# One 512-column fp32r matmul per direction for the decay rows of an mLSTM mixer, with operands of 128 rows in place of 64

## The chip, the cores and the metric

The kernel runs on one core of a Trainium2 chip. The metric is the device time of one execution in microseconds (us), as the median of several runs. The work is latency-bound inference of a small batch: 256 tokens of 1024 numbers, with about 320 MB of float32 weights that are read from HBM once.

## The reference, cut to what matters

Two layers: the first is a bidirectional mLSTM mixer and a PEER feed-forward part, the second a differential attention mixer and another PEER part. The change is in the first mixer. In one direction and for one head it computes, in chunks,

```python
D = b[..., :, None] - b[..., None, :] + li[..., None, :]     # decay from s to t
D = jnp.where(mask, D, -jnp.inf)
m_t = jnp.maximum(g, jnp.max(D, axis=-1))
Sqk = jnp.einsum('bhctd,bhcsd->bhcts', q, k) * jnp.exp(D - m_t[..., None])
num = jnp.einsum('bhcts,bhcsv->bhctv', Sqk, v) + ...          # state of the chunks before
h = num / jnp.maximum(jnp.abs(den), jnp.exp(-m_t))[..., None]
```

and h_fwd + h_bwd goes on, normalised by head, gated by sigmoid(o), and through w_out. The kernel does without chunks: it treats all 256 positions as one, so that for each head and direction there is one 256 x 256 matrix exp(A_s - M_t), masked, times the scores k_s.q_t, and one product with v.

## The kernel before, in words

**Weights.** All weight matrices are one stream of 128 x 1024 units (512 KB), in the order in which TensorE uses them: gate (1 unit), qk (8), vo (16), wo0 (8), wq0 (16), u0 and v0 (128 each), then the second layer's. SyncE loads each unit into a ring of four slots (`raw`). ScalarE rounds it to fp32r (`wh`, L465), VectorE makes the rest (`wl = raw - wh`, L826), and TensorE multiplies with both, so that three fast fp32r products stand for one float32 product. ScalarE and VectorE go ahead of TensorE by three units; the calls `ahead(unit)` in their programs say at which point the next unit is split. TensorE adds to the semaphore `used` behind each unit, and that frees the slot.

**The order of work is written out by hand** for each engine, in program order, with semaphores between the engines. There is no planner around the change.

**Start of the first mixer.** After the first norm, VectorE splits its units, clears three small tiles (L893 to L895; `zrow` is a row of zeros that a scan at L933 uses later, on partitions 0 to 15), copies the transposed gate projection out of PSUM (L897, `gT`), and TensorE transposes `gT` back between the first two qk units (L1530). The gates' logarithms are summed on 16 partitions (8 heads, 2 directions), and the results are turned into `colC` and `colD` (per token, one column per head and direction) and into `rowM`: for each direction and head the row -M_t over the 256 tokens. `rowM` has 64 rows in fp32r: rows 0 to 31 hold the rounded values, rows 32 to 63 what rounding left (L962, L963). `pick` (L948, L949) has 16 columns with ones in row c and row 32 + c, so that `pick[:, c]` as stationary operand, repeated over 128 columns, times `rowM` gives row c, to nearly full float32 precision, on all 128 partitions.

**The heads.** TensorE's loop over the eight heads (L1629) is: `o_unit(h)`, one weight unit of the gate o (12 matmuls of 512 columns, L1502 to L1504); `ml_decay(h + 1)`; after odd h `ml_scores` of the next two heads (L1596, 64-row float32 matmuls); `ml_values(h)` (L1622, six float32 products, which the profile shows as twelve matmuls). Before the loop stand `ml_decay(0)` and `ml_scores(0)`. In `ml_decay`, for each direction (PSUM bank 2 forward, bank 3 backward) and each half s of the source tokens, one fp32r matmul of 64 rows and 256 columns writes the picked row (L1609), and one bf16 matmul of 128 columns adds the triangle of -1e30 to the diagonal block (L1611):

```python
for b, c, m in ((2, h, mask_f), (3, 8 + h, mask_b)):
    for s in range(NT):
        at_ = s * S + s * P
        pe.matmul(ps[:, b, s * S:(s + 1) * S], pick[0:64, c:c + 1].to_broadcast([64, P]), rowM[0:64, :],
                  start=True, stop=False)
        i = pe.matmul(ps[:, b, at_:at_ + P], ident_b[:], m[:], start=False, stop=True)
i.then_inc(decay_mm, 1)
```

`ml_exp` on ScalarE (L549 to L552) waits for `decay_mm` and takes exp of the banks with the token's column of `colC` or `colD` as bias; `ml_weights` on VectorE (L975) multiplies by the scores; `ml_den` (L986 to L995) makes the denominators of the head before, ScalarE scales its forward part (L558), and `ml_output` (L1002) adds the backward part and signals `hs_ready`, for which `ml_values` of the next head waits. In heads 5 and 6 VectorE also gates finished heads (`ml_gate`, L1011), in head 6 it prepares the norm (L857), and in head 7 it scales the first four heads (L873), which TensorE then transposes (L1452). `v_block` (L944) copies v out of the banks that the first decay block then overwrites.

The full-width weight passes elsewhere serve the prediction as measures: `up_both_halves` (L1483 to L1486, fp32r, 128 rows, 512 and 256 columns), `weights` in the feed-forward part (L1678, f16, 128 rows, 64 columns), `keep_warm` (L1431, bf16, 512 columns, one operand repeated by a zero step), and the small products L1530 (32 rows) and L1580 (64 stationary columns).

Of the kernel before, what the change touches and what calls it, by code (L numbers as in the profile page):

```python
# [44 lines left out]
P = 128  # L45
S = 256
D = 1024
NT = S // P
# [51 lines left out]
def program(nc, stream, small, keys0, keys1, positions, x_in, out):  # L100
    with ExitStack() as ctx:
        def sb(name, shape, dt=F32):
            return ctx.enter_context(nc.sbuf_tensor(name, shape, dt))
# [4 lines left out]
        ps = ctx.enter_context(nc.psum_tensor("ps", [P, 8, 512], F32))  # L108
# [13 lines left out]
        ident_b = sb("ident_b", [P, P], BF16)  # L122
# [13 lines left out]
        rowM = sb("rowM", [P, S], F32R)  # L136
        pick = sb("pick", [P, 16], F32R)

        def area(at, *shape, dt=F32):

            n = int(np.prod(shape))
            v = big[:, at:at + (n // 2 if dt in (BF16, F16) else n)]
            if dt != F32:
                v = v.bitcast(dt)
            names = "abcd"[:len(shape)]
            if len(shape) > 1:
                v = v.rearrange(f"p ({' '.join(names)}) -> p {' '.join(names)}",
                                **{k: s for k, s in zip(names, shape)})
            return v
# [19 lines left out]
        zrow = area(18160, S)  # L169
# [613 lines left out]
        def _(dve):  # L783
            steps = [0]

            def chain(ins):

                steps[0] += 1
                ins.then_inc(dve_step, 1)
                dve.wait_ge(dve_step, steps[0])  # L790
# [100 lines left out]
            transposed(0, gain(0))  # L891
            ahead(0)
            dve.memset(v_ml[:, :, :, P:P + 1], 1.0)  # L893
            dve.memset(zrow[0:16, :], 0.0)
            chain(dve.memset(lgate[:], 0.0))  # L895
            dve.wait_ge(used, unit_of["gate"] + 1)
            dve.tensor_copy(gT[0:32, :], ps[0:32, 7, 0:S]).then_inc(gT_ready, 1)  # L897
            ahead(unit_of["qk"])
# [12 lines left out]
            for t in range(NT):  # L911
                i = dve.scalar_tensor_tensor(out=ftmp[:, 0, t], in0=g4[:, t, :, 1, :], scalar=-1.0,
                                             in1=g4[:, t, :, 1, :], op0=ALU.mult, op1=ALU.max)
# [8 lines left out]
            for d in range(2):  # L922
                i = dve.scalar_tensor_tensor(out=lgate[:, :, 2 + d, 8 * d:8 * d + 8], in0=g4[:, :, d, 1, :], scalar=0.0,
                                             in1=ftmp[:, 2, :, d, :], op0=ALU.min, op1=ALU.subtract)
# [32 lines left out]
            for d, col in ((0, colC), (8, colD)):  # L957
                i = dve.tensor_copy(colM[:, :, 0:3:2, d:d + 8],
                                    col[:, :, 16 + d:24 + d].unsqueeze(2).to_broadcast([P, NT, 2, 8]))
# [322 lines left out]
            for k in range(ROPE_HALF):  # L1282
                i = dve.tensor_scalar(trig[:, 1, :, k], trig[:, 0, :, 0], float(ROPE_INV[k]), None, ALU.mult)
# [138 lines left out]
        def _(pe):  # L1422
# [118 lines left out]
            for k in range(2):  # L1541
                for t in range(NT):
                    at_ = k * S + t * P
                    pe.matmul(ps[0:16, 7, at_:at_ + P], lgate[:, t, 2 * k, :], ident[:], start=True, stop=False)
                    i = pe.matmul(ps[0:16, 7, at_:at_ + P], lgate[:, 1 - t, 2 * k + 1, :], flip[:],
                                  start=False, stop=True)
# [19 lines left out]
            for t in range(NT):  # L1566
                for k in range(3):
                    at_ = t * 48 + k * 16
                    i = pe.matmul(ps[:, 7, at_:at_ + 16], rows[0:16, k, t * P:(t + 1) * P], ident[0:16, 0:16],
                                  start=True, stop=True)  # L1570
# [3 lines left out]
            for t in range(NT):  # L1574
                i = pe.matmul(ps[:, 7, t * 48:(t + 1) * 48], flip[:], colC[:, 1 - t, :], start=True, stop=True)
# [3 lines left out]
            for t in range(NT):  # L1579
                i = pe.matmul(ps[0:64, 7, t * P:(t + 1) * P], colM[:, t].rearrange("p r c -> p (r c)"), ident[:],  # L1580
                              start=True, stop=True)
# [18 lines left out]
            def ml_decay(h):  # L1600

                if h == 0:
                    pe.wait_ge(v_out, 4)
                else:
                    pe.wait_ge(e_ready, h)
                for b, c, m in ((2, h, mask_f), (3, 8 + h, mask_b)):
                    for s in range(NT):
                        at_ = s * S + s * P
                        pe.matmul(ps[:, b, s * S:(s + 1) * S], pick[0:64, c:c + 1].to_broadcast([64, P]), rowM[0:64, :],  # L1609
                                  start=True, stop=False)  # L1610
                        i = pe.matmul(ps[:, b, at_:at_ + P], ident_b[:], m[:], start=False, stop=True)  # L1611
                i.then_inc(decay_mm, 1)

            def ml_values(h):
# [10 lines left out]
                i.then_inc(av_mm, 1)  # L1625

            ml_decay(0)
            ml_scores(0)
            for h in range(HEADS):  # L1629
                o_unit(h)  # L1630
                if h + 1 < HEADS:
                    ml_decay(h + 1)
                if h % 2 == 1 and h + 1 < HEADS:
                    ml_scores((h + 1) // 2)
                if h == HEADS - 1:
                    pe.wait_ge(e_ready, HEADS)
                    for pair in range(2):
                        head_transposes(1, pair)
                ml_values(h)
# [246 lines left out]
```

## Time and profile before

| | |
|---|---|
| median of three runs | 1892.0 us (1890.98 to 1892.17) |
| the profiled execution's own time | 1889.36 us |
| its span | 1887.6 us |
| mean granted TensorE clock | 0.997 of full |
| busy: TensorE, VectorE, ScalarE, GpSimd | 99%, 76%, 52%, 6% |
| HBM traffic | 325 MB, 172 GB/s over the span |
| the eight heads of the first mixer | from 68.7 to 123.2 us |

The profile is of one execution. A matmul's record covers its way through the array, so records overlap; where TensorE is never idle, the distance between two starts tells what a matmul costs. "PEld" is the load of the stationary operand, which can run beside the matmul ahead of it.

### The profile page before, as it was taken

How to read it: one execution, taken by the hardware profiler on the slowest of the kernel's cores; microseconds unless marked ns; L12 is line 12 of the kernel's file. 1: busy time of each engine (PE TensorE's matmuls, PEld its weight loads, DVE VectorE, ACT ScalarE, POOL GpSimd, SP SyncE). 2: the span in 40 equal slices, each digit the busy share in tenths (PEclk: the TensorE clock that was granted, in tenths of full speed). 3: DMA queues.
4: the chain of work that ended last, by engine and by line, in shares of the span. 5: the costliest groups of instructions: out<-in, count | busy, mean ns of one | idle time of the engine just before them, and what ended most of it. 6: DMA issues, size and time to landing. Idle time of an engine off the chain costs nothing.

```text
span 1887.6 us, 33014 instructions
## 1 busy us (share of the span) xinstructions
PE 1862.8 (99%) x11274; PEld 1563.4 (83%) x11274; DVE 1428.1 (76%) x2630; ACT 978.9 (52%) x1398; POOL 105.9 (6%) x71
## 2 busy tenths in 40 slices
PE   8999999999999999999999999999999999999998
PEld 6778888888888888888876688888888888888887
DVE  5566588988888888655578756889888888885555
ACT  5465555655554444444466655555555444444444
POOL 0000342000000000000000003410000000000000
PEclk9999999999999999999999999999999999999999
DMA  6335455555555555555554244555555555555554
GB/s 228 123 112 167 156 191 189 177 172 175 171 174 179 176 173 173 190 193 192 193 175 137 88 159 163 182 189 178 178 178 170 171 172 172 174 176 195 194 193 163
DMA packets 89487, 326.13 MB, mean 173 GB/s; under 512 B 10065, under 2 KB 10193, under 8 KB 89041
## 3 DMA queue, kind: packets, MB, share of 16 engines
q1 hardware_dynamic: 88848, 323.00, 52.4%
q10 hardware_dynamic: 576, 2.33, 0.3%
q8 instruction: 35, 0.57, 0.1%
q14 instruction: 28, 0.22, 0.0%
HBM read 324.24 MB, written 1.05 MB: 172 GB/s over the span
## 4 chain that ended last, share of the span: by engine, by line
PE 94%; DVE 3%; ACT 2%; issue 0%; DMA 0%; DVEq 0%; ACTq 0%
PE ps L1486 25%; PE ps L1484 14%; PE ps L1730 12%; PE ps L1732 12%; PE ps L1731 12%; PE ps L1483 4%; PE ps L1678 3%; PE ps L1502 2%; PE ps L1504 2%; PE ps L1503 2%; DVE wl L826 1%; PE ps L1659 1%; PE ps L1622 1%; PE ps L1609 1%; ACT big L483 0%; ACT big L752 0%
## 5 line engine op out<-in xcount | busy, mean ns | idle before, releaser
L826 DVE TENSOR_TENSOR wl<-raw,wh 128x1024 fp32r<-128x1024 f32 x572 | 699.5, 1226 | 167.9 <-ACT wh L465 159.2
L465 ACT ACTIVATE wh<-raw 128x1024 fp32r<-128x1024 f32 x612 | 644.9, 1055 | 323.5 <-PE ps L1732 171.1
L1486 PE MATMUL ps<-hT,wh 128*128 128x512 f32 x2072 | 737.7, 396 | 0.0
L1484 PE MATMUL ps<-hT,wl 128*128 128x256 f32 x2368 | 612.9, 279 | 0.0
L1484 PEld LDWEIGHTS ps<-hT,wl 128*128 128x128 f32 x2368 | 446.7, 189 | 24.8
L1486 PEld LDWEIGHTS ps<-hT,wh 128*128 128x128 f32 x2072 | 389.7, 188 | 78.3
L1730 PE MATMUL ps<-wh,hT 128*128 128x512 f32 x1024 | 402.3, 393 | 0.4 <-DVE big L810 0.4
L1732 PE MATMUL ps<-wh,hT 128*128 128x512 f32 x1024 | 399.4, 390 | 0.0
L1731 PE MATMUL ps<-wl,hT 128*128 128x512 f32 x1024 | 398.8, 389 | 0.0
L1732 PEld LDWEIGHTS ps<-wh,hT 128*128 128x128 f32 x1024 | 192.3, 188 | 40.4
L1730 PEld LDWEIGHTS ps<-wh,hT 128*128 128x128 f32 x1024 | 192.5, 188 | 39.6 <-issue 1.0
L1731 PEld LDWEIGHTS ps<-wl,hT 128*128 128x128 f32 x1024 | 192.6, 188 | 39.0
L675 ACT ACTIVATE hT<-big 128x512 fp32r (+1 forms) x128 | 80.8, 632 | 221.2 <-PE ps L1732 212.4
L632 ACT ACTIVATE big<-ps 128x512 f32 (+1 forms) x128 | 76.6, 598 | 224.3 <-PE ps L1486 224.3
L1238 DVE TENSOR_TENSOR hT<-big,hT 128x512 fp32r<-128x512 f32 x128 | 88.2, 689 | 117.1 <-ACT hT L675 117.1
L423 POOL TENSOR_TENSOR wl<-raw,wh 128x1024 fp32r<-128x1024 f32 x40 | 96.5, 2413 | 1122.2 <-ACT wh L465 1122.2
L1483 PE MATMUL ps<-hT,wh 128*128 128x512 f32 x296 | 120.7, 408 | 2.2 <-DVE hT L836 1.4
L1191 DVE SCALAR_TENSOR_TENSOR big<-ps,big 128x512 f32 (+1 forms) x128 | 87.5, 685 | 35.0 <-PE ps L1678 30.9
L810 DVE TENSOR_TENSOR big<-ps,big 128x512 f32<-128x512 f32 (+1 forms) x128 | 87.7, 685 | 31.6 <-ACT big L632 31.1
L1502 PE MATMUL ps<-wh,hT 128*128 128x512 f32 x224 | 89.4, 399 | 0.7 <-DVE hT L836 0.7
L1175 DVE TENSOR_TENSOR hots_i<-iota_h,slot_d 128x1024 f16<-128x1024 f16 x128 | 87.4, 683 | 0.0
L1504 PE MATMUL ps<-wh,hT 128*128 128x512 f32 x224 | 87.4, 390 | 0.0
(224 smaller groups left out, 1359.4 us busy)
## 6 DMA issues: line engine op xcount, KB each, us to landing
raw<-stream SPq DMA_DIRECT2D x612, 512.0 KB, 3.4
big<-keys ACTq DMA_DIRECT2D x2, 1024.0 KB, 7.7
x<-x_in SPq DMA_DIRECT2D x1, 1024.0 KB, 5.5
out<-x SPq DMA_DIRECT2D x4, 256.0 KB, 2.2
sm<-small ACTq DMA_DIRECT2D x1, 228.5 KB, 5.7
pos_i<-positions ACTq DMA_DIRECT2D x1, 1.0 KB, 6.6
```

Source lines behind the costliest of these rows:

```text
L423: pool.tensor_tensor(wl[:, r, :], raw[:, r, :], wh[:, r, :].bitcast(F32), ALU.subtract).then_inc(low_odd, 1)
L465: act.activation(wh[:, r, :], raw[:, r, :], ACT.Copy).then_inc(high_ready, 1)
L826: dve.tensor_tensor(wl[:, r, :], raw[:, r, :], wh[:, r, :].bitcast(F32), ALU.subtract).then_inc(made_low(unit), 1)
L1238: dve.tensor_tensor(stage_l[:, pair % 2, :], G[:, bass.ds(offset(turn, TURN, 2 * pair), 2), :].rearrange("p j t -> p (j t)"), stage_h[:, p ...
L1483: pe.matmul(wide, w_h[:, kd, :], both, start=True, stop=False)
L1484: pe.matmul(near, w_l[:, kd, :], hTh[:, kd, :], start=False, stop=False)
L1486: i = pe.matmul(wide, w_h[:, kd, :], both, start=False, stop=(kd == KD - 1))
L1502: pe.matmul(out(t), h_h, w_h[:, k, :], start=(kd == 0), stop=False)
L1504: i = pe.matmul(out(t), h_l, w_h[:, k, :], start=False, stop=(kd == KD - 1))
L1730: pe.matmul(out_, g_h, w_h[:, cols], start=fresh_bank, stop=False, skip_group_check=True)
L1731: pe.matmul(out_, g_h, w_l[:, cols], start=False, stop=False, skip_group_check=True)
L1732: i = pe.matmul(out_, g_l, w_h[:, cols], start=False, stop=False, skip_group_check=True)
```

## The change

`rowM` and `pick` get their rows 64 to 127 filled with zeros, once, early in VectorE's program. For each direction of a head, one matmul with 128 rows and 512 columns replaces the two with 64 rows and 256 columns: its moving operand is `rowM` read twice by a zero step, and it writes the whole bank. The two mask matmuls of the direction follow it; the accumulation group is closed by the second.

```diff
             ahead(0)
             dve.memset(v_ml[:, :, :, P:P + 1], 1.0)
-            dve.memset(zrow[0:16, :], 0.0)
+            dve.memset(zrow[:], 0.0)
             chain(dve.memset(lgate[:], 0.0))
+            dve.tensor_copy(rowM[64:P, :], zrow[64:P, :])
+            dve.tensor_copy(pick[64:P, :], zrow[64:P, 0:16])
             dve.wait_ge(used, unit_of["gate"] + 1)
             dve.tensor_copy(gT[0:32, :], ps[0:32, 7, 0:S]).then_inc(gT_ready, 1)
             ahead(unit_of["qk"])
...
                 for b, c, m in ((2, h, mask_f), (3, 8 + h, mask_b)):
+                    pe.matmul(ps[:, b, :].rearrange("p (s t) -> p s t", s=NT), pick[:, c:c + 1].to_broadcast([P, P]),
+                              rowM[:].unsqueeze(1).to_broadcast([P, NT, S]), start=True, stop=False)
                     for s in range(NT):
                         at_ = s * S + s * P
-                        pe.matmul(ps[:, b, s * S:(s + 1) * S], pick[0:64, c:c + 1].to_broadcast([64, P]), rowM[0:64, :],
-                                  start=True, stop=False)
-                        i = pe.matmul(ps[:, b, at_:at_ + P], ident_b[:], m[:], start=False, stop=True)
+                        i = pe.matmul(ps[:, b, at_:at_ + P], ident_b[:], m[:], start=False, stop=(s == NT - 1))
                 i.then_inc(decay_mm, 1)
```

## Rows read from the trace of the kernel before

**Rows 1.** The page: busy time by engine, and the last chain by engine.

```profile
PE 1862.8 (99%) x11274; PEld 1563.4 (83%) x11274; DVE 1428.1 (76%) x2630; ACT 978.9 (52%) x1398; POOL 105.9 (6%) x71
...
PE 94%; DVE 3%; ACT 2%; issue 0%; DMA 0%; DVEq 0%; ACTq 0%
```

**Rows 2.** TensorE's waits, 64 to 126 us: in total, times, longest.

```profile
PE ps L1609 <- DVE big L944: 1.3, 1, 1.3
PE ps L1622 <- DVE big L1002: 0.4, 1, 0.4
```

**Rows 3.** Timeline of one decay block: start us, length us, engine, line, operation, shapes, count.

```profile
87.41 0.39 PE L1503 MATMUL ps<-wl,hT 128*128 128x512 f32 x1
87.41 0.19 PEld L1504 LDWEIGHTS ps<-wh,hT 128*128 128x128 f32 x1
...
87.63 0.39 PE L1504 MATMUL ps<-wh,hT 128*128 128x512 f32 x1
87.95 0.18 PEld L1609 LDWEIGHTS ps<-rowM,pick 64*128 64x128 f32 x1 [0.35 <-issue]
...
88.27 0.23 PE L1611 MATMUL ps<-big,ident_b 128*128 128x128 bf16 x1
88.42 0.18 PEld L1609 LDWEIGHTS ps<-rowM,pick 64*128 64x128 f32 x1
...
89.68 0.23 PE L1611 MATMUL ps<-big,ident_b 128*128 128x128 bf16 x1
89.75 1.56 PE L1622 MATMUL ps<-big 128*128 128x129 f32 x12
```

**Rows 4.** Timeline: changes of type with 128 rows on both sides, and L1431.

```profile
499.92 0.40 PE L1486 MATMUL ps<-hT,wh 128*128 128x512 f32 x1
500.15 1.11 PE L1678 MATMUL ps<-hots_j,hots_i 128*128 128x64 f16 x32
501.10 0.47 PE L1483 MATMUL ps<-hT,wh 128*128 128x512 f32 x1
...
1082.41 2.33 PE L1431 MATMUL ps<-ident_b 128*128 128x512 bf16 x10
```

**Rows 5.** Timeline around L1580: the way into 64 stationary columns, and a bare load.

```profile
60.81 0.39 PE L1504 MATMUL ps<-wh,hT 128*128 128x512 f32 x1
61.13 0.41 PEld L1580 LDWEIGHTS ps<-ident,big 128*64 128x64 f32 x4 [0.35 <-issue]
...
61.71 0.19 PEld L1502 LDWEIGHTS ps<-wh,hT 128*128 128x128 f32 x1 [0.17 <-issue]
...
61.82 0.19 PEld L1503 LDWEIGHTS ps<-wl,hT 128*128 128x128 f32 x1
...
62.05 0.40 PE L1503 MATMUL ps<-wl,hT 128*128 128x512 f32 x1
```

**Rows 6.** Timeline: VectorE at L897 and L962, and TensorE's way into L1530.

```profile
19.52 0.41 DVE L897 COPY big<-ps 32x256 f32<-32x256 f32 x1
...
20.24 0.40 PE L1486 MATMUL ps<-hT,wh 128*128 128x512 f32 x1
20.57 0.20 PEld L1530 LDWEIGHTS ps<-ident,big 32*128 32x128 f32 x2 [0.25 <-issue]
...
61.82 0.42 DVE L962 CAST rowM<-ps 64x256 fp32r<-64x256 f32 x1 [2.75 <-PE ps L1580]
```

**Rows 7.** Timeline: TensorE and VectorE in head 6, and a wake-up in head 7.

```profile
110.23 1.61 PE L1622 MATMUL ps<-big 128*128 128x129 f32 x12
...
114.19 0.39 PE L1504 MATMUL ps<-wh,hT 128*128 128x512 f32 x1
114.44 0.61 DVE L1002 SCALAR_TENSOR_TENSOR big<-ps,big 128x128 f32<-128x128 f32 x2
...
121.14 0.60 DVE L1002 SCALAR_TENSOR_TENSOR big<-ps,big 128x128 f32<-128x128 f32 x2
121.88 1.58 PE L1622 MATMUL ps<-big 128*128 128x129 f32 x12 [0.39 <-DVE big L1002]
```

## The prediction

> **What bounds the kernel now.** I read the page's busy shares and its chain first: TensorE is busy for 99% of the span and makes 94% of the chain that ended last [rows 1]. A step saved on TensorE is therefore worth its own length, if nothing else on its path ends later. The second view is the list of waits for the stretch 64 to 126 us, which holds the eight heads of the first mixer [rows 2]. TensorE waits there twice: 1.3 us ahead of the first decay block for VectorE's copy of v, and 0.4 us ahead of one ml_values. The other seven decay blocks wait for no engine. The third view is the timeline of one head [rows 3]. What to see in it is not the duration of an instruction, which overlaps the next one, but the distance from one start to the next.
>
> **How a decay block spends its time.** Inside o_unit the starts are 0.22 us apart (87.41, 87.63), and the load for L1504 starts with the matmul before it (87.41): loads are hidden. At the decay block that ends. From L1504 to the first load of L1609 it is 0.32 us, 0.09 more than the 0.23 that 512 columns take. A load of L1609 now starts with its own matmul instead of one matmul earlier. From L1609 to L1611 it is 0.32 us (87.95 to 88.27), from L1611 to L1609 0.15; a round is 0.47 (87.95 to 88.42), and there are four per head: 1.88 us. From L1504's start at 87.63 to the first ml_values matmul at 89.75 it is 2.12 us [rows 3].
>
> Which of two things costs this, the 64 rows or the change of type between fp32r and bf16? Rows with 128 rows on both sides of a change of type answer it. From L1486 (fp32r, 512 columns) to the f16 matmuls of L1678 it is 0.23 us (499.92 to 500.15), with nothing on top. L1611 to L1622, bf16 to fp32, both with 128 rows, is 0.07 (89.68 to 89.75), half of the 0.15 to the 64-row L1609 [rows 3, 4]. And where the type is not the reason but the shape of the weights changes (L1504 to L1580, 64 columns; L1486 to L1530, 32 rows), the distance is 0.32 and 0.33 again, after a matmul of 0.23 [rows 5, 6]. So I read the extra 0.1 us at each change as the price of changing the part of the array that is used, paid eight times per head now (once on the way in, four times into the masks, three times back). The changed block has 128 rows and 128 columns throughout, and pays it nowhere, except at the way into ml_scores, as before.
>
> The Trainium skill says the same in "TensorEngine Tiling (Array Packing)", Key Properties: changing the tiling mode drains TensorE. Its page "TensorE: Matmul & The Clock Gate", Part 3, has a rule that speaks against this change: a load overlaps a running matmul only where their row groups differ. By it the 128-row block would hide none of its loads; that is the first rival below. The trace disagrees: L1504's load and the matmul before it use the same 128 rows and start together.
>
> **The change, part by part.** Per head, two matmuls of 512 columns take the place of four of 256, and four mask matmuls stay.
> - The 512-column fp32r matmul takes 0.23 us, as L1486 does before L1678 [rows 4].
> - From the first mask matmul to the second: 32 f16 matmuls of 64 columns go in 0.95 us (500.15 to 501.10), 0.03 each [rows 4]. Twice the columns: 0.06, an estimate. Ends: 0.03, and the 0.15 that L1611 takes today.
> - From the second mask to the next fp32r matmul: its load of 128 columns cannot hide behind a 0.06 matmul. A bare load is 0.11 (61.71 to 61.82, where nothing stands ahead of it) [rows 5]. I take 0.11; ends 0.07 (L1611 to L1622) and 0.15.
> - Per head, counted from the last L1504 of o_unit: its own 0.23, then 0.23 + 0.06 + 0.11 for one direction, 0.23 + 0.06 for the other, and 0.07 to L1622: 0.99 us in place of 2.12. The saving is 1.13 us. It holds where ml_scores follows, since the way into its 64-row matmuls is the same before and after. Seven heads: 7.9 us.
> - Head 0 comes behind a wait, not behind L1504. Before, four rounds: 1.88 from its first load. After: 0.11 + 0.23 + 0.06 + 0.11 + 0.23 + 0.06 + 0.15 = 0.95, so 0.9 us.
> - The masks' and the zeros' arithmetic costs TensorE nothing beyond this: 32 matmuls and 32 loads fall to 16 each.
> - VectorE gains two copies at 19.5 us, between the clearing of lgate and the copy of gT (L897), and a memset that is wider in partitions only, which I cost at nothing, since its free size is the same. The copy of 64 x 256 is at most L962's 0.42, which reads PSUM; the one of 64 x 16 is small, 0.1 to 0.2. Both together: 0.3 to 0.6 us. Queued behind them: L897, which now ends at 19.93, then the weight split of the next unit, then the gate's arithmetic. TensorE waits for gT at the transposes L1530, which start at 20.57, and the matmul before them starts at 20.24 [rows 6]. VectorE's delay puts L897's end at 20.2 to 20.5, a wake-up later (about 0.1) it is 20.3 to 20.6: it costs 0 to 0.1 us, I take 0.05. The gate's own results are wanted by TensorE only at 40 us, after seven more units, so their half microsecond is covered by the work on qk.
>
> Sum: 7.9 + 0.9 - 0.05 = 8.75, say 8.8 us. No DMA and no weight unit is added or moved; the ring's loads simply follow TensorE sooner.
>
> **Is another engine the bound once TensorE is faster?** Each ml_values needs hs_ready of the head before, VectorE's L1002, whose chain starts at the previous ml_values. The tightest turn is head 6, in which VectorE also gates two heads: ml_values starts at 110.23, the last L1504 at 114.19, L1002 ends at 115.05, and a wake-up costs 0.14 (121.74 to 121.88) [rows 7]. VectorE's side is ready at 115.19, TensorE's new side at 114.19 + 0.99 = 115.18. That is a tie, and costs 0.01 us. The next thing to be late is this chain. It would cost whatever VectorE is slower than in this run. The other heads lack the gating or have ml_scores in front. Head 7 has no decay block behind its o_unit, and its wait for VectorE moves along with the ml_values of head 6.
>
> **The numbers.** The durations are from one profiled execution of 1889.36 us with a span of 1887.6. The median of the three timed runs is 1892.0, 2.6 above it, and they spread over 1.2 us. The sum gives a span of 1878.8 and a time of 1883.2 against the median. I call 0.2% (3.8 us) what a measurement of this kernel can tell from no change.
>
> **Rivals.**
> 1. Changing between fp32r and bf16 stalls in any shape, and the load is never hidden in the decay block. Then the 512-column matmul is 0.32 + 0.11 (the second 256 columns, half of 0.23) = 0.43, the mask pair 0.06, the way on 0.15: 0.64 per direction and 1.28 per head in place of 1.88. Saved: 0.6 x 8 = 4.8 us, 1887.2. For it: every change of type inside today's block stalls. Against it: the undisturbed changes at 128 rows [rows 4]. Chance 0.13.
> 2. The chains of VectorE and ScalarE (denominators, gating, the reload of the exp table in head 7) end last in heads 5 to 7, and only the first five heads keep their gain: 0.9 + 4 x 1.13 = 5.4 us, 1886.6. For it: the tie in head 6, and the one wait of 0.4 us. Against it: nothing in heads 1 to 4 or 7 is near. Chance 0.07.
> 3. Slower: reading rowM twice by a zero step in the 512-column fp32r matmul runs at a quarter of the rate. Its place is each L1609 of the new kernel. Its price: 0.91 in place of 0.23, 0.68 x 16 = 10.9 us, so 8.8 saved turns into 2.1 lost, 1894.1. It decides from 0.78 us per matmul on (0.55 x 16 = 8.8). Against it: the bf16 matmuls of L1431 read their operand four times by a zero step, and ten of them go in 2.33 us, which with a tail of 0.4 on the last leaves 0.21 to 0.22 each, the full rate [rows 4]; for it only that no fp32r row has such a step. Chance 0.03.
>
> The forecast has the remaining 0.77. Its own range is 1881.8 to 1884.5 (mask step 0.03 to 0.10, load 0.07 to 0.15, and the spread of the runs). Rivals 1 and 2 are taken in on the upper side: 1881.5 to 1887.5. Faster 0.92 (forecast, rival 2, and most of rival 1, whose 4.8 us is just above the bound), same 0.05, slower 0.03.
>
> **What would show it right or wrong.** In the changed kernel's timeline: L1504 to the new matmul 0.23, not 0.32; the new matmul to its first mask 0.23; mask to mask 0.06; a decay block of some 0.75 us. A distance of 0.42 there is rival 1; of over 0.7, rival 3. ml_values starting only behind L1002 in heads 1 to 5 is rival 2. At 20.5 us TensorE's gap ahead of L1530 should grow by less than 0.1. Everything from 126 us on should look the same, earlier by 8.8. I am wrong if the block shrinks as said and the span does not: then a later stage is not bound by TensorE as the page says.

## The result, and the profile after

| | before | changed |
|---|---|---|
| median of five runs | 1890.98 us (1889.50 to 1892.17) | 1880.92 us (1879.62 to 1882.96) |
| ratio, with its 95% interval | | 0.9946 (0.9935 to 0.9957) |
| the profiled execution's own time, its span | 1889.36, 1887.6 | 1882.96, 1881.1 |

Three single runs (one of e5, one of e9, one of the kernel before) took 2633, 4760 and 7199 us, far above all the others, and are left out of every median, mean and comparison.

The change takes 10.1 us off by the medians, 8.1 to 12.3 by the interval. The forecast was 8.8 off and 1883.2 us, with a range of 1881.5 to 1887.5. The direction is right, the saving is near, and the time lies 0.6 us below the range. Meanwhile the two profiled executions are only 6.4 us apart. So there are three numbers for one change, 6.4, 8.8 and 10.1, and the question is which of them is the decay blocks.

The page of the changed kernel, busy time and chain, as [rows 1]. (Lines behind the diff have moved by two: L1504 to L1506 are now o_unit's matmuls, L1613 the masks, L1624 ml_values, L1004 ml_output.)

```profile
PE 1855.8 (99%) x11258; PEld 1560.3 (83%) x11258; DVE 1429.3 (76%) x2632; ACT 978.8 (52%) x1398; POOL 105.9 (6%) x71
...
PE 94%; DVE 3%; ACT 2%; issue 0%; DMA 0%; DVEq 0%; ACTq 0%
```

TensorE's busy time fell by 7.0 us, and it is still the bound. Its waits from 64 to 126 us answer to [rows 2] and are the same two, of the same length:

```profile
PE ps L1609 <- DVE big L946: 1.3, 1, 1.3
PE ps L1624 <- DVE big L1004: 0.4, 1, 0.4
```

The timeline of the same decay block as in [rows 3]:

```profile
86.61 0.39 PE L1506 MATMUL ps<-wh,hT 128*128 128x512 f32 x1
86.62 0.19 PEld L1609 LDWEIGHTS ps<-rowM,pick 128*128 128x128 f32 x1
86.84 0.40 PE L1609 MATMUL ps<-rowM,pick 128*128 128x512 f32 x1
...
87.08 0.28 PE L1613 MATMUL ps<-big,ident_b 128*128 128x128 bf16 x2
87.14 0.19 PEld L1609 LDWEIGHTS ps<-rowM,pick 128*128 128x128 f32 x1
87.17 0.48 PE L1609 MATMUL ps<-rowM,pick 128*128 128x512 f32 x1
...
87.49 0.29 PE L1613 MATMUL ps<-big,ident_b 128*128 128x128 bf16 x2
87.56 1.42 PEld L1624 LDWEIGHTS ps<-big 128*128 128x128 f32 x12
87.62 1.56 PE L1624 MATMUL ps<-big 128*128 128x129 f32 x12
```

From the last matmul of o_unit to ml_values it is 1.01 us (86.61 to 87.62) where it was 2.12; 0.99 was forecast. The load of pick now starts with the matmul before it (86.62), the way in is 0.23, and the wide matmul reaches its masks in 0.24. The second load is not hidden: its matmul's record starts at 87.17, but the masks follow only 0.32 later, 0.09 more than 512 columns take. Over the heads, from the first L1609 (68.8 before, 70.9 changed) to the first matmul of wo0 (123.2 and 116.6) it was 54.4 us and is 45.7: 8.7 saved.

Why then only 6.4 between the two profiled executions? Busy time by engine and granted clock (PEclk) in the stretch 8 to 17 us, the kernel before and then the changed one:

```profile
core 0: us, PE busy (x) PEld busy (x) DVE busy (x) ACT busy (x) POOL busy (x), PEclk, DMA share, GB/s
8.00:17.00 9.00, 6.16 (x36) 5.36 (x36) 7.83 (x18) 7.61 (x17) 0.00 (x0) 0.81 0.92 340
```

```profile
core 0: us, PE busy (x) PEld busy (x) DVE busy (x) ACT busy (x) POOL busy (x), PEclk, DMA share, GB/s
8.00:17.00 9.00, 6.28 (x27) 5.69 (x28) 7.88 (x18) 7.55 (x17) 0.00 (x0) 0.59 0.87 334
```

TensorE's clock falls to its lower level around the idle time of 2 to 2.6 us that ends at 10.2 in both (low from 10.9 to 14.3 before, from 9.6 to 19.8 changed), so in this execution of the changed kernel it stays there through the gate unit. The gate unit starts at 14.6 in both; the heads' stage begins 2.1 us later. 8.7 less 2.1 is 6.6. Two more differences of about 1 us nearly cancel: the second layer's attention is 1.0 us shorter in the changed kernel's profile, and its weights part 1.1 us longer (both are told with e8). No instruction up to the heads was changed on TensorE. What is left to explain is the other side: why the timed runs show about 10.

### The profile page after: what moved, and what is told of

It reads as the page before. It is cut to its first block, busy times and chain, and to the rows that moved or that the text cites. A ratio compares the mean times of both kernels' runs of the same rounds, so it can differ in the third digit from the quotient of the medians.

```text
span 1881.1 us, 32983 instructions
## 1 busy us (share of the span) xinstructions
PE 1855.8 (99%) x11258; PEld 1560.3 (83%) x11258; DVE 1429.3 (76%) x2632; ACT 978.8 (52%) x1398; POOL 105.9 (6%) x71
## 4 chain that ended last, share of the span: by engine, by line
PE 94%; DVE 3%; ACT 2%; issue 0%; DMA 0%; DVEq 0%; ACTq 0%
PE ps L1488 25%; PE ps L1486 14%; PE ps L1732 13%; PE ps L1734 12%; PE ps L1733 12%; PE ps L1485 4%; PE ps L1680 3%; PE ps L1504 2%; PE ps L1506 2%; PE ps L1505 2%; DVE wl L826 1%; PE ps L1661 1%; PE ps L1624 1%; ACT big L483 0%; ACT big L752 0%
## 5 line engine op out<-in xcount | busy, mean ns | idle before, releaser
L1732 PE MATMUL ps<-wh,hT 128*128 128x512 f32 x1024 | 402.2, 393 | 0.3 <-DVE big L810 0.2
L1734 PE MATMUL ps<-wh,hT 128*128 128x512 f32 x1024 | 399.3, 390 | 0.0
L1504 PE MATMUL ps<-wh,hT 128*128 128x512 f32 x224 | 89.4, 399 | 0.7 <-DVE hT L836 0.7
L1182 DVE TENSOR_TENSOR hots_j<-same_j,gate_d 128x1024 f16<-128x1024 f16 x128 | 87.7, 685 | 0.0
```

Of the source, the lines that this page charges most:

```text
L1504: pe.matmul(out(t), h_h, w_h[:, k, :], start=(kd == 0), stop=False)
L1732: pe.matmul(out_, g_h, w_h[:, cols], start=fresh_bank, stop=False, skip_group_check=True)
L1734: i = pe.matmul(out_, g_l, w_h[:, cols], start=False, stop=False, skip_group_check=True)
```

## The experiments

**e1, the changed kernel again**, without an edit.

> The changed kernel, unaltered, timed again beside the kernel before. Theory A: the change is worth what the stretch of the eight heads shows in the two profiles (54.4 us before, 45.7 after: 8.7 us), and the rest of the first comparison (10.1 us between the medians) is the TensorE clock at the start of the kernel, which falls to its lower level at a point that differs from run to run. Then the ratio is 0.9954, with single runs of either kernel some 2 to 3 us apart, and a run's time goes with its mean granted clock (0.997 to 0.999). Theory B: the change is worth more outside the heads. Then the ratio is 0.9946 or less again.

Ratio 0.9946 (0.9934 to 0.9959); medians 1882.15 and 1892.08. Theory B's number came out twice, but not its reason: outside the start and the heads, the lengths of the parts take the same few values in both kernels (193.3 to 193.4 us from the first score matmul to the weights part in every profile; the others are told with e8). And the spread of single runs is as theory A has it: the changed kernel's six runs lie between 1880.8 and 1884.7 (0.999 to 0.997 of full clock), the kernel before from 1889.6 to 1895.1. Over all timed runs of this study the mean of the kernel before is 1891.6 us (48 runs, standard error 0.2) and that of the changed kernel 1881.9 (11 runs, 0.5): 9.7 us apart, give or take 0.6. One run's time is thus no measure of 1 us; the lengths of stages in the traces are, and the next three experiments are read there.

**e2, the rows alone**: zeros and 128 rows, 256 columns.

```diff
-                        pe.matmul(ps[:, b, s * S:(s + 1) * S], pick[0:64, c:c + 1].to_broadcast([64, P]), rowM[0:64, :],
+                        pe.matmul(ps[:, b, s * S:(s + 1) * S], pick[:, c:c + 1].to_broadcast([P, P]), rowM[:],
```

> The zeros and 128 rows, but still two 256-column matmuls per direction. Theory A (changing the used part of the array stalls, a change of type does not): from the last matmul of the gate unit to the first ml_values matmul it is 0.23 + 0.12 + 3 x (0.07 to 0.09 + 0.20) + 0.07, so 1.2 to 1.3 us in place of 2.12 before and 1.01 in the changed kernel; about 6.5 to 7 us faster than before. Rival (a change of type stalls in any shape): each round stays at 0.47 and the block at 2.0 to 2.1; within 1 us of before.

Timeline of a decay block of e2 (L1611 is the picking matmul here):

```profile
84.90 0.39 PE L1506 MATMUL ps<-wh,hT 128*128 128x512 f32 x1
85.12 0.28 PE L1611 MATMUL ps<-rowM,pick 128*128 128x256 f32 x1
85.24 0.23 PE L1613 MATMUL ps<-big,ident_b 128*128 128x128 bf16 x1
85.28 0.36 PE L1611 MATMUL ps<-rowM,pick 128*128 128x256 f32 x1
85.49 0.23 PE L1613 MATMUL ps<-big,ident_b 128*128 128x128 bf16 x1
...
86.05 1.56 PE L1624 MATMUL ps<-big 128*128 128x129 f32 x12
```

and its loads there:

```profile
85.24 0.10 PEld L1613 LDWEIGHTS ps<-big,ident_b 128*128 128x128 bf16 x1 [0.15 <-issue]
85.25 0.20 PEld L1611 LDWEIGHTS ps<-rowM,pick 128*128 128x128 f32 x1
85.49 0.10 PEld L1613 LDWEIGHTS ps<-big,ident_b 128*128 128x128 bf16 x1
```

The block takes 1.15 us, a little less than the 1.2 to 1.3 expected, and a round 0.25 (85.24 to 85.49) where it was 0.47, with the same four changes of type. Ratio 0.9953 (0.9939 to 0.9967). So a change between fp32r and bf16 does not stall when both use 128 rows: the first rival is refuted. (The rows at L1580 and L1530, from which the prediction read this, change from fp32r to fp32 together with the shape; this pair of kernels changes the rows alone.) The Trainium skill's rule in "TensorEngine Tiling (Array Packing)", Key Properties, that changing the tiling mode drains TensorE, agrees with this pair of rounds. The other rule, of "TensorE: Matmul & The Clock Gate", Part 3, that loads overlap only between different row groups, does not: e2's load at 85.25 and the changed kernel's at 86.62 overlap the matmuls before them within the same 128 rows.

**e3, the width alone**: one 512-column matmul on 64 rows, no zeros.

```diff
+                    pe.matmul(ps[:, b, :].rearrange("p (s t) -> p s t", s=NT), pick[0:64, c:c + 1].to_broadcast([64, P]),
+                              rowM[0:64].unsqueeze(1).to_broadcast([64, NT, S]), start=True, stop=False)
```

> One 512-column matmul per direction, but with 64 rows as before and no zeros. Theory A: the stall of 0.1 us stays at each change between 64 and 128 rows and the loads stay uncovered: 0.32 on the way in, then per direction 0.43 for the wide matmul, 0.06 between the masks and 0.15 (0.07 at the end): a block of 1.5 us in place of 2.12; 4.8 us faster than before, about half of the change. Rival (the number of matmuls is all, rows count for nothing): a block of 1.0 us as in the changed kernel, 8.7 us faster.

```profile
87.17 0.39 PE L1504 MATMUL ps<-wh,hT 128*128 128x512 f32 x1
87.48 0.18 PEld L1607 LDWEIGHTS ps<-rowM,pick 64*128 64x128 f32 x1 [0.35 <-issue]
...
87.91 0.29 PE L1611 MATMUL ps<-big,ident_b 128*128 128x128 bf16 x2
88.13 0.18 PEld L1607 LDWEIGHTS ps<-rowM,pick 64*128 64x128 f32 x1
...
88.56 0.29 PE L1611 MATMUL ps<-big,ident_b 128*128 128x128 bf16 x2
88.63 1.42 PEld L1622 LDWEIGHTS ps<-big 128*128 128x128 f32 x12
88.68 1.56 PE L1622 MATMUL ps<-big 128*128 128x129 f32 x12
```

1.51 us, of which 0.31 is the way in and 0.43 each wide matmul, as expected; ratio 0.9961 (0.9946 to 0.9975). A wide matmul of 64 rows takes 0.2 us longer to its mask than the first one of the changed kernel (0.43 against 0.24): by the prediction's terms 0.1 for its uncovered load and 0.1 for the stall, which this pair does not separate.

**e4, the zeros alone**: the three edits of VectorE's program, the old blocks.

> The zero rows are written (the wider memset and the two copies), but the decay matmuls stay as before. Theory A: VectorE's copies at 19.5 us take 0.3 and 0.2 us, TensorE's transposes of the gate rows start at most 0.1 us later behind their neighbours, and the time stays within 0.5 us of before, apart from what the clock does at the start. Rival: the half microsecond is passed on through the gate's chain, 0.5 us slower.

Ratio 0.9996 (0.9987 to 1.0005). VectorE's timeline in e4 shows what the two copies take:

```profile
19.51 0.29 DVE L896 CAST rowM<-big 64x256 fp32r<-64x256 f32 x1
19.72 0.17 DVE L897 CAST pick<-big 64x16 fp32r<-64x16 f32 x1
19.90 0.41 DVE L899 COPY big<-ps 32x256 f32<-32x256 f32 x1
```

The copy of gT starts 0.38 us later than in [rows 6], which is what 0.3 to 0.6 allowed. In e2, where the clock rose as early as in the first profile, the product of the gate rows (L1546 there, L1544 before) starts at 40.6 us as before: the delay costs nothing.

But e4's profile showed what the first one did not: a lower clock among the heads. It is told with e10.

**The stages of all profiles.** The first column after the name is the stretch near the start in which the granted clock was at its lower level. Then come the start of the rowM product (L1580 before) and that of the first score matmul of the feed-forward part (L1659 before). Between these two lie the heads, wo0 and wq0, and nothing of the start.

| kernel | lower clock before 20 us | rowM product | first score matmul | between | less than 136.0 |
|---|---|---|---|---|---|
| before | 10.9 to 14.3 | 61.1 | 197.2 | 136.0 | |
| changed | 9.6 to 19.8 | 63.3 | 190.6 | 127.3 | 8.7 |
| e1, changed | 15.2 to 18.6 | 62.6 | 189.9 | 127.3 | 8.7 |
| e2, rows only | 10.9 to 14.3 | 61.1 | 189.6 | 128.5 | 7.5 |
| e3, width only | 11.3 to 18.1 | 62.5 | 193.6 | 131.2 | 4.9 |
| e4, zeros only | 11.5 to 18.4 | 62.6 | 200.2 | 137.6 | -1.6 |
| e6, changed, filled wait | 15.8 to 19.2 | 62.4 | 189.6 | 127.2 | 8.8 |
| e7, reordered | 10.0 to 13.4 | 61.1 | 187.9 | 126.8 | 9.3 |
| e8, changed, warm start | none | 61.2 | 188.5 | 127.3 | 8.7 |
| e10, before | 11.2 to 18.0 | 62.5 | 200.0 | 137.5 | -1.5 |
| e11, before | 10.8 to 14.2 | 61.1 | 197.2 | 136.0 | 0 |
| e13, before | 11.4 to 18.2 | 62.5 | 200.1 | 137.6 | -1.6 |
| e14, before | 15.3 to 18.7 | 62.4 | 198.4 | 136.0 | 0 |

(Lengths and differences are taken before rounding.) The decay blocks are worth 8.7 us, where 8.8 was forecast, in the profiles of the changed kernel against those of the kernel before with full clock. And the kernel before has a second value, 137.5 to 137.6.

**e10, e11, e13 and e14, the kernel before, four more profiles.**

> The kernel before, profiled a second time, to see how often its clock falls among the eight heads. Theory A (the fall behind the wait for v is frequent in it and accounts for what the change gave beyond 8.8 us): a lower clock for some 3.4 us between 68 and 85 us in about half of such looks, and then 137.5 instead of 136.1 us from the rowM product to the first score matmul. Theory B: none.

> As e10: a third profile of the kernel before. Theory A: in one of the two there is a lower clock between 68 and 85 us. Theory B: in neither.

> A fourth profile of the kernel before. So far a lower clock among the heads in one of its three, and in one of one of the kernel with the zeros alone, which has the same decay blocks; in none of seven profiles of kernels with 128-row blocks. Theory A (it falls there in about half of the executions): one more in the two looks e13 and e14, and each execution with it has 137.5 instead of 136.1 us from the rowM product to the first score matmul. Theory B (chance): none in either.

> As e13: a fifth profile of the kernel before. Theory A: a lower clock among the heads in one of the two. Theory B: in neither.

e10 and e13 have it, e11 and e14 have not, as theory A expected. The clock is at its lower level from 72.6 to 76.1 us in e10, from 72.8 to 76.2 in e13 and from 73.0 to 76.4 in e4. Busy time and granted clock in e10:

```profile
core 0: us, PE busy (x) PEld busy (x) DVE busy (x) ACT busy (x) POOL busy (x), PEclk, DMA share, GB/s
60.00:68.00 8.00, 8.00 (x38) 6.23 (x37) 5.08 (x9) 2.62 (x3) 0.00 (x0) 1.00 0.20 61
68.00:72.00 4.00, 2.67 (x14) 1.46 (x12) 1.96 (x3) 0.00 (x0) 0.00 (x0) 1.00 0.97 305
72.00:76.00 4.00, 4.00 (x15) 2.83 (x15) 2.28 (x5) 2.30 (x5) 0.00 (x0) 0.58 0.26 101
```

and TensorE's timeline there:

```profile
73.41 0.79 PE L1502 MATMUL ps<-wh,hT 128*128 128x512 f32 x1
74.00 0.63 PE L1503 MATMUL ps<-wl,hT 128*128 128x512 f32 x1
74.42 0.63 PE L1504 MATMUL ps<-wh,hT 128*128 128x512 f32 x1
...
76.11 0.39 PE L1502 MATMUL ps<-wh,hT 128*128 128x512 f32 x1
...
77.58 0.38 PE L1609 MATMUL ps<-rowM,pick 64*128 64x256 f32 x1
```

Behind the 1.3 us wait for v and the first decay block the starts are 0.42 us apart, which is 512 columns at 1.2 GHz, and 0.23 again from 76.1 on. That o_unit takes 4.2 us where it takes 3.0 in the first profile:

```profile
71.73 0.50 PE L1502 MATMUL ps<-wh,hT 128*128 128x512 f32 x1
...
74.69 0.38 PE L1609 MATMUL ps<-rowM,pick 64*128 64x256 f32 x1
```

With the old blocks and the wait as it was, three of six profiles have this fall (e4, e10, e13); with 128-row blocks none of seven has (the changed kernel, e1, e2, e6 to e9). Half of 1.5 us is 0.75, and 8.7 + 0.75 = 9.45 lies within the 9.7, give or take 0.6, of the means; 8.7 alone is not excluded by them either.

But the three against none does not compare like with like. All three profiles with the fall have one and the same start, the lower clock from about 11.3 to 18.1 us; the other three of those six had another start, and no fall. None of the seven profiles with 128-row blocks had that start, and in two of them (e6, e9) the wait was filled. So these seven do not show that the 128-row block prevents the fall. The profiles that do share that start are e15, e3 and e16, and they are the ones to read against e4, e10 and e13.

**e5, e12 and e15, the kernel before with its wait filled.**

```diff
+            pe.wait_ge(v_out, 2)
+            keep_warm(0, 5)
             ml_decay(0)
             ml_scores(0)
```

> The kernel before, with five bf16 matmuls of 512 columns on bank 0 in the 1.3 us in which TensorE waits for v ahead of the first decay block. Theory A: in some executions of the kernel before, TensorE's clock falls to its lower level behind that wait and the stalling blocks after it (in the profile with the zeros alone it did: 0.5 from 72.7 to 76.1 us, and the o_unit there took 4.3 instead of 3.0 us). Filling the wait removes that: no profile shows a lower clock between 60 and 125 us, and the mean of its runs is 0.3 to 1.2 us below the kernel before. Theory B (the fall behind the wait is a rarity that does not count in the means): within 0.3 us.

> The kernel before with the filled wait, profiled again, since the first profile of it fell in an execution whose clock was 0.65 throughout. Theory A: full clock from 25 us to the second layer's attention. Theory B: a fall among the heads all the same, so that the stalling blocks and not the wait bring it about.

> The kernel before with the filled wait, once more. If the 1.3 us of idle time is needed for the fall, none, as in e12; if the stalls of the 64-row blocks suffice, a fall among the heads.

Ratio 0.9995 (0.9986 to 1.0004), so the timing alone does not decide. The mean of e5's eleven runs, 1890.3 us, is 1.1 below that of the kernel before beside it, with a standard error of 0.5, which leans towards theory A. The execution that e5's profile caught had a granted clock of 0.65 nearly throughout, so its lengths are not used. It has a fall to 0.5 as well, from 71.2 to 74.6 us, but there that is ahead of the heads, among the v units. e12 and e15 have full clock from 60 to 125 us, 136.0 us between the two marks, and single times of 1889.3 and 1891.0. e15 is the telling one: its start is like e10's and e13's, with the same PEclk of 0.69 from 8 to 19 us and the rowM product at 62.5, and where those two fell it does not:

```profile
core 0: us, PE busy (x) PEld busy (x) DVE busy (x) ACT busy (x) POOL busy (x), PEclk, DMA share, GB/s
68.00:72.00 4.00, 3.86 (x18) 1.90 (x17) 2.02 (x3) 0.00 (x0) 0.00 (x0) 1.00 0.84 269
72.00:76.00 4.00, 4.00 (x21) 2.85 (x20) 2.28 (x5) 2.30 (x5) 0.00 (x0) 1.00 0.35 142
```

**e6, the changed kernel with the same filling.**

> The changed kernel with the same five matmuls in its wait. Theory A: the shorter decay and the earlier dense work already keep the clock up there, so nothing is gained: within 0.3 us of the changed kernel, and 8.7 us below the filled kernel before, which would be the plain worth of the decay blocks. Theory B: it keeps the 10 us to the kernel before and 10 to the filled one.

Ratio 0.9948 (0.9934 to 0.9962), median 1880.93 beside 1891.01 of the kernel before: the filling adds nothing to the changed kernel, and its stage is 127.2. Between the filled pair, e5 and e6, the medians are 9.6 apart and the means 9.2, not 8.7; with a spread of 2.7 us among e6's five runs this does not separate the theories.

**e16, the width alone, profiled again.**

> The 512-column matmuls with 64 rows once more. Its heads are between the two kernels (131.1 us from the rowM product to the first score matmul). A fall among the heads would say that the stalls at 64 rows bring it about; none, as in e3, leaves it open.

No fall, and 131.2 us between the marks (62.5 to 193.7), with a start like e13's. In e3 and e16 the wait is not filled and the rows are 64; only the block is shorter by 0.6 us. With this start, then, the fall came in all three profiles with the unfilled wait and the long block, not in the two with the shorter block, and not in the one with the wait filled. That speaks for both being needed, on six profiles; with the changed kernel's own block this start was never seen.

**e7, both wide matmuls first, then the four masks.**

```diff
                 for b, c, m in ((2, h, mask_f), (3, 8 + h, mask_b)):
                     pe.matmul(ps[:, b, :].rearrange("p (s t) -> p s t", s=NT), pick[:, c:c + 1].to_broadcast([P, P]),
                               rowM[:].unsqueeze(1).to_broadcast([P, NT, S]), start=True, stop=False)
+                for b, c, m in ((2, h, mask_f), (3, 8 + h, mask_b)):
                     for s in range(NT):
```

> The changed kernel with both wide matmuls of a head first and then its four masks, so that the second load of pick hides behind the first wide matmul. From the changed kernel's trace: mask to wide matmul 0.09 and wide matmul to mask 0.31 to 0.32 become wide to wide 0.23, and then 0.23 to the masks; masks 0.05 to 0.06 apart. The block falls from 1.01 to 0.9 us: 0.9 us over eight heads, below what the timing can tell alone. If the 0.31 is not the exposed load, the block stays at 1.0.

```profile
84.27 0.39 PE L1506 MATMUL ps<-wh,hT 128*128 128x512 f32 x1
84.50 0.63 PE L1609 MATMUL ps<-rowM,pick 128*128 128x512 f32 x2
84.97 0.40 PE L1614 MATMUL ps<-big,ident_b 128*128 128x128 bf16 x4
85.20 1.56 PE L1625 MATMUL ps<-big 128*128 128x129 f32 x12
```

The block is 0.93 us, 0.08 less: two wide matmuls in 0.47 and four masks in 0.23, 0.06 each. So the 0.09 between the two directions of the changed kernel is the load of pick, which nothing hides behind two short masks. The stage is 0.6 us shorter (126.75 against 127.31); the ratio, 0.9947 (0.9932 to 0.9962), cannot show it.

**e8, a longer warm start of the changed kernel**: 18 bf16 matmuls instead of 12, and two more behind the first transposes.

> The changed kernel with 18 instead of 12 bf16 matmuls at its start, and two more behind the first transposes, so that TensorE has less idle time before the gate unit. Theory A: the clock's fall at 9 to 11 us, which lasts to 14.4 us in one profile and to 19.8 in another, accounts for most of the 2 to 5 us by which single runs differ; with it gone or shorter the runs lie within some 2 us, the mean clock is 0.998 to 0.999, and the median is 1 to 2 us below the changed kernel. Rival: the spread comes from elsewhere (the second layer's attention, the DMA), and neither median nor spread changes.

Half of it came. The clock stays at its upper level through to the end of the kernel (mean 1.0), and the rowM product starts at 61.2 instead of 62.6 to 63.3. But the median is 1880.85, not 1 to 2 us lower, and the runs still spread over 2.4 us, so the start is one source of the spread and not the whole of it. The traces show three more. The stretch with the second layer's attention, from the last transposes of q and k (L1766) to the last score matmul, takes 122.3 to 122.4 us in the profiles with full clock there (changed, e11) and 123.2 to 123.5 in those with a lower clock for 3.4 us (before, e1, e10, e14); in e9 the lower clock lasts 6.8 us, and the stretch 124.5. And from the first weights product (L1678) to the first down product (L1730) it is 189.7 us in most (before, changed) and 190.9 in others (e1, e3, e4, e10, e11), at full clock: between the changed kernel's profile and e1 the difference grows evenly, some 0.02 us per unit, and TensorE waits for no engine there longer than 0.2 us. The same part of the second layer takes the same two values, not always together with the first: 189.7 before and in e1, 190.9 in the changed kernel, e2 and e4. What sets that was not tried.

**e9, all three**: reordered, filled, warm start.

> The changed kernel with the reordered decay block, the filled wait and the longer warm start together: the candidate that should beat both. From the profiles so far: 8.8 us for the decay blocks, 0.5 for the order, and 0 to 2 for the start. Theory A: mean of its runs 10.5 to 11.5 us below the kernel before, 0.5 to 1.5 below the changed kernel, no lower clock anywhere before the second layer's attention. Rival (the additions only fill idle time that was free): the same as the changed kernel.

Ratio 0.9941 (0.9928 to 0.9954); the median is 1880.24 beside 1891.28. The time between the marks is 126.7 (61.1 to 187.8), 0.6 below the changed kernel. It had full clock up to the attention. Its five runs average 1880.6, which is 11.0 below the kernel before and 1.3 below the changed kernel, with a standard error of 0.8 on the latter. It is the best candidate, and it is not shown to be faster than the changed kernel.

## Why the prediction was right and wrong

**The bound, right.** TensorE is the bound in the heads, and what is taken from the block arrives at the end of the stage in full.

**The price of 64 rows, right.** The stall goes with the change of the rows used and not with the change of type. e2 and e3 separate the parts: rows alone save 7.5 us, width alone 4.9, both 8.7. They overlap: with fewer matmuls there are fewer crossings left for the 128 rows to remove. The padding that computes nothing is the larger part.

**The terms, right.** Block 0.99 forecast, 1.01 measured; head 0 0.95 forecast, 0.97 (its first load at 70.91, the first score matmul at 71.88); mask to mask 0.06, as e7 shows; the load behind the masks 0.11 forecast, 0.09 found. Copies 0.3 to 0.6 us, 0.38 found, cost 0.05 forecast and none found.

**The tie in head 6, right.** There L1506 starts at 108.70 and ml_values at 109.71, 1.01 as elsewhere, while VectorE's L1004 ends at 109.56:

```profile
108.70 0.39 PE L1506 MATMUL ps<-wh,hT 128*128 128x512 f32 x1
...
108.95 0.61 DVE L1004 SCALAR_TENSOR_TENSOR big<-ps,big 128x128 f32<-128x128 f32 x2
...
109.71 1.58 PE L1624 MATMUL ps<-big 128*128 128x129 f32 x12
```

That is also the limit of this line of work: a still shorter block meets this chain in head 6. Rival 2 did not happen, rival 1 fell with e2, rival 3 with the 0.24 of the wide matmul.

**The step that failed** is the one in "The numbers", where the durations of one profiled execution were set against the median of three runs, and the range got 1.2 us for the spread. Two things are wrong in it. The kernel's runs differ by 5.6 us (1889.5 to 1895.1 over 48 of them), and two more of them already moved the median before from 1892.0 to 1890.98. Against that median the sum would have given 1882.2, and a range lowered by the same 1.0 us would have held the measured 1880.92. And the sum holds for one clock history only. In three of six profiles the kernel before (or its twin e4) loses 1.5 us among the heads to a clock that has fallen behind the wait and the long block. The first profile had none of it by luck, its granted clock is 1.00 throughout the stage, and no term was made for it. If the change takes this away, it is worth about 0.75 us in the mean. That is not shown: the 128-row kernels were never seen with the start that went with every fall, and only e3 and e16, with a shorter block of 64 rows, bear on it. How much of the 10.1 beyond 8.7 is this fall and how much the spread of five runs stays open. That the saving of 8.8 came out at 8.7 in the traces is no luck: the parts were each measured and agree; that the timed medians came near it owes something to it, since one median moves by 1 us with two more runs.

## What to carry to other kernels

A matmul with fewer rows or columns than its neighbours may cost more than one with all 128: here 0.1 us at each crossing and its load uncovered, so zero rows pay for themselves when the small matmul stands between full ones, and the order should put wide matmuls next to each other so that a load hides behind one. (Whether the 64-row matmuls, put together ahead of the masks, would have saved as much was not tried.) Read the distance between starts, not the durations. Before giving a range for a kernel whose runs differ by more than the change, measure lengths of stages in several profiles, and read the granted clock behind every wait of TensorE.

## What had not been expected of the hardware

- Behind a wait of 1.3 us on TensorE and a block of stalling small matmuls, its clock was at 1.2 GHz (granted 0.5) for some 3.4 us in three of six profiles with the same TensorE program, the three in which it had also been low from about 11.3 to 18.1 us, and not in the others.
- The same part of the feed-forward stage took one of two lengths, 189.7 or 190.9 us, in both layers and both kernels, with full clock and without a wait that explains it.
- With 128 rows on both sides, the record of a bf16 mask matmul of 128 columns is followed by that of an fp32r matmul 0.04 us later (85.24 to 85.28 in e2), and the load's cost appears only at the matmul after it (0.21 us to 85.49, where 256 columns without it take 0.12, from 85.12 to 85.24).
